# Decoder trunk on one core: the second layer's mixer norm by token on turned residual rows, top two by index instruction

## The chip, the core and the metric

The kernel runs on one NeuronCore of one Trainium2 chip. The metric is the device time of one execution in microseconds (us); lower is better. Before the change three runs gave a median of 1497.2 us (1497.12 to 1497.33).

## The reference, cut to what matters

Two layers over 288 tokens (256 of a prompt, 8 x 4 samples) of width 1024, all in float32. Layer 0 has a dense feed-forward, layer 1 routes each token to two of eight experts:

```python
h = layer_norm(ALPHA * h + mix, p['ln_mix_g'][i], p['ln_mix_b'][i])
flat = h.reshape(bsz * L, D_MODEL)
...
    f = moe_swiglu(flat, p['w_router'][j], p['w_e_gate'][j], p['w_e_up'][j], p['w_e_down'][j])
h = layer_norm(ALPHA * h + f.reshape(bsz, L, D_MODEL), p['ln_ffn_g'][i], p['ln_ffn_b'][i])
...
def moe_swiglu(h, w_router, w_gate, w_up, w_down):
    logits = (h @ w_router).astype(jnp.float32)
    top_logit, top_e = lax.top_k(logits, TOP_K)
    gates = jax.nn.softmax(top_logit, axis=-1).astype(h.dtype)
...
        return (jax.nn.silu(xb @ w_gate[e]) * (xb @ w_up[e])) @ w_down[e]
...
    return jnp.zeros((T, D), h.dtype).at[sorted_tok].add(y_assign * w_assign[:, None])
```

`layer_norm(x, g, b)` is `(x - mean) * rsqrt(var + 1e-5) * g + b` over the 1024 channels of a token.

## The kernel before

**Layout.** Activations lie channel by token: `h` and `r` are eight blocks (k) of 128 channels x 288 tokens. Every fp32 weight chunk (1 MB) comes through a ring of six buffers, loaded on SyncE's queue (SP), and is split in two fp32r halves: ScalarE (ACT) copies `w_hi`, VectorE (DVE) subtracts for `w_lo` (three slots each). TensorE (PE) multiplies hi by hi, hi by lo and lo by hi. All orders are written out by hand, engine by engine, with semaphores.

**From the second mixer to the experts** (layer 1; the place of the change). PE projects the mixer's output block by block (L691); DVE adds `ALPHA*h` to give `r` (L1393) and keeps a running sum of the blocks (L1400). Then comes a norm over channels, which lie on partitions: PE sums with a matrix of ones (L519, L523), DVE centres eight blocks (L1314), ACT squares them (L1027), PE sums the squares (L538), DVE takes the variance off the diagonal (L1377), GpSimd (POOL) takes the power of -0.5 (L2039), PE spreads the result over all partitions (L547), DVE multiplies (L1683), ACT applies the vectors g and b (L1152). PE turns the finished `h` into rows by token (L806), ACT and DVE split those into `h_tok_hi` (L1210) and `h_tok_lo` (L1749). Beside this PE computes the router's logits on the centred `r` (L793), and DVE finds the two largest with 14 small operations, each waiting for the one before (L1719 to L1740).

**Selection and gathering.** PE counts each chosen token's place in its expert (L829 to L831); DVE compares the places with a row of slot numbers (L1765), which gives `sel`, a 0/1 matrix of tokens by slots for the experts 0 and 1. PE gathers their tokens with `sel` in four pieces q of two channel blocks (L845), ACT and DVE split each piece into `x_hi` (L1218) and `x_lo` (L1884). PE starts expert 0 (item 0) when two pieces are there and its chunk 1 when all four are. `keep_warm` (L507) is a run of matmuls whose result nobody reads.

**The experts.** Each of the eight items is 42 chunks p in seven groups g. For every chunk from p = 2 ACT cuts `w_hi` (L1253), then DVE `w_lo` (L1940). The generator `extra_items` hands DVE one small piece of other work behind each cut of item 0 (`beside`): among it the sum of the two halves to plain rows `x_rows` (L1803, L1813) and the start of the result `r_tok` (L1798). POOL stores `x_rows` to DRAM (L2114), from where the later experts' tokens are fetched.

## Time and profile before

| | |
|---|---|
| median of three runs | 1497.2 us |
| the profiled execution, its own time | 1497.28 us |
| its span on the core | 1495.5 us |
| PE busy | 1481.0 us, 99% |
| DVE, ACT, POOL busy | 82%, 64%, 6% |
| granted TensorE clock, mean | 0.999 |

A span is the time from the first to the last record of the core; the execution's own time has 1.8 us more around it. An engine is busy while an instruction of it runs. A matmul's record is longer than the distance to the next one, since matmuls are pipelined, so distances between starts tell more. A wait is named by what ended it.

### The profile page before, as it was taken

What the parts mean: (1) busy time and instruction counts of PE and PEld (TensorE: products, weight loads), DVE (VectorE), ACT (ScalarE), POOL (GpSimd) and SP (SyncE); (2) the same over time, 40 slices, a digit from 0 to 9 for tenths busy, and PEclk for the clock granted to TensorE, in tenths of its full rate; (3) what the DMA queues carried; (4) which work ended last, traced back from release to release, by engine and by line L of the source; (5) the groups of instructions that cost most, each with busy time, mean ns of one, the idle gap of its engine ahead of it and who ended that gap; (6) DMA issues with size and microseconds to landing.
All of it is one profiled execution on the core that took longest, in us unless ns stands there. A gap on an engine that the chain in (4) does not pass through costs nothing.

```text
span 1495.5 us, 20554 instructions
## 1 busy us (share of the span) xinstructions
PE 1481.0 (99%) x7975; PEld 1285.3 (86%) x7975; DVE 1231.3 (82%) x1260; ACT 957.0 (64%) x891; POOL 94.8 (6%) x104
## 2 busy tenths in 40 slices
PE   9999999999999999999999999999999999999998
PEld 8989999999998788888888888888888888788887
DVE  7977655554697788899999988898889889999886
ACT  5734433344374477777777777777777777677774
POOL 3402000000021000001000000100000101100000
PEclk9999999999999999999999999999999999999999
DMA  9725544454251479999999999999999999999991
GB/s 346 160 78 190 182 158 166 169 169 169 85 130 57 169 285 399 374 390 373 421 376 369 378 390 381 392 366 375 371 366 403 375 398 380 408 371 358 379 378 69
DMA packets 68154, 439.43 MB, mean 294 GB/s; under 512 B 9504, under 2 KB 13536, under 8 KB 16608
## 3 DMA queue, kind: packets, MB, share of 16 engines
q1 hardware_dynamic: 60320, 424.68, 74.8%
q0 software_dynamic: 4816, 12.32, 2.7%
q10 hardware_dynamic: 2928, 1.18, 0.3%
q8 instruction: 63, 1.03, 0.3%
q14 instruction: 27, 0.22, 0.0%
HBM read 431.06 MB, written 7.09 MB: 293 GB/s over the span
## 4 chain that ended last, share of the span: by engine, by line
PE 94%; DVE 3%; ACT 1%; issue 1%; DMA 0%; DVEq 0%; POOL 0%; SPq 0%; ACTq 0%; POOLq 0%
PE bank L885 60%; PE bank L557 23%; PE bank L691 4%; PE bank L928 2%; PE bank L507 1%; PE bank L581 1%; DVE w_lo L1940 1%; PE bank L538 1%; DVE w_lo L1326 0%; ACT w_hi L1055 0%; PE bank L547 0%; PE bank L523 0%; PE bank L875 0%; PE bank L866 0%; DVE r L1393 0%
## 5 line engine op out<-in xcount | busy, mean ns | idle before, releaser
L1940 DVE TENSOR_TENSOR w_lo<-ring,w_hi 128x2048 fp32r<-128x2048 f32 x320 | 731.2, 2290 | 84.2 <-ACT w_hi L1253 81.7
L1253 ACT ACTIVATE w_hi<-ring 128x2048 fp32r<-128x2048 f32 x320 | 613.5, 1918 | 163.0 <-PE bank L885 163.0
L885 PE MATMUL bank<-w_hi,x_hi 128*128 128x512 f32 x896 | 354.2, 395 | 0.9 <-DVE w_lo L1940 0.8
L885 PE MATMUL bank<-w_hi,x_lo 128*128 128x512 f32 x896 | 349.6, 390 | 0.0
L885 PE MATMUL bank<-w_lo,x_hi 128*128 128x512 f32 x896 | 348.9, 389 | 0.0
L557 PE MATMUL bank<-x_hi,w_hi 128*128 128x290 f32 x664 | 199.5, 300 | 0.6 <-DVE w_lo L1326 0.5
L885 PEld LDWEIGHTS bank<-w_hi,x_lo 128*128 128x128 f32 x896 | 168.2, 188 | 35.7
L885 PEld LDWEIGHTS bank<-w_hi,x_hi 128*128 128x128 f32 x896 | 168.4, 188 | 35.3 <-issue 1.9
L557 PE MATMUL bank<-x_lo,w_hi 128*128 128x290 f32 x664 | 197.7, 298 | 0.0
L557 PE MATMUL bank<-x_hi,w_lo 128*128 128x290 f32 x664 | 197.3, 297 | 0.0
L885 PEld LDWEIGHTS bank<-w_lo,x_hi 128*128 128x128 f32 x896 | 168.5, 188 | 33.3
L1326 DVE TENSOR_TENSOR w_lo<-ring,w_hi 128x2048 fp32r<-128x2048 f32 x60 | 137.2, 2289 | 34.3 <-ACT w_hi L1055 31.3
L1055 ACT ACTIVATE w_hi<-ring 128x2048 fp32r<-128x2048 f32 x60 | 114.0, 1905 | 53.6 <-PE bank L557 44.2
L557 PEld LDWEIGHTS bank<-x_hi,w_hi 128*128 128x128 f32 x664 | 126.0, 190 | 2.0 <-DVE w_lo L1326 1.1
L557 PEld LDWEIGHTS bank<-x_lo,w_hi 128*128 128x128 f32 x664 | 126.3, 190 | 0.3
L557 PEld LDWEIGHTS bank<-x_hi,w_lo 128*128 128x128 f32 x664 | 126.0, 190 | 0.0
L885 PE MATMUL bank<-w_hi,ad_hi 128*128 128x512 f32 x256 | 100.4, 392 | 0.1
L885 PE MATMUL bank<-w_hi,ad_lo 128*128 128x512 f32 x256 | 99.8, 390 | 0.0
L885 PE MATMUL bank<-w_lo,ad_hi 128*128 128x512 f32 x256 | 99.7, 390 | 0.0
L885 PE MATMUL bank<-w_hi,odd_hi 128*128 128x512 f32 x192 | 75.6, 394 | 0.0
L885 PE MATMUL bank<-w_hi,odd_lo 128*128 128x512 f32 x192 | 74.9, 390 | 0.0
L885 PE MATMUL bank<-w_lo,odd_hi 128*128 128x512 f32 x192 | 74.8, 389 | 0.0
(300 smaller groups left out, 1759.7 us busy)
## 6 DMA issues: line engine op xcount, KB each, us to landing
ring<-in_w_e_gate SPq DMA_DIRECT2D x112, 1024.0 KB, 7.1
ring<-in_w_e_up SPq DMA_DIRECT2D x112, 1024.0 KB, 7.1
ring<-in_w_e_down SPq DMA_DIRECT2D x112, 1024.0 KB, 7.3
ring<-in_w_in SPq DMA_DIRECT2D x16, 1024.0 KB, 5.9
ring<-in_w_ff_gate SPq DMA_DIRECT2D x14, 1024.0 KB, 5.0
ring<-in_w_ff_up SPq DMA_DIRECT2D x14, 1024.0 KB, 5.0
ring<-in_w_ff_down SPq DMA_DIRECT2D x14, 1024.0 KB, 4.9
...
```

The lines of the kernel that those rows point to most:

```text
L507: mm(bank[b][:, 384:512], ones[:, :], ones[:, :], start=True, stop=True)
L538: last = mm(bank[7][:, 0:TOKENS], ones[:, :], sq[:, b, :], start=(b == 0), stop=(b == nb - 1))
L557: ins = mm(out, w, x, start=(first and n == 0), stop=(last and n == 2), skip_group_check=True)
L581: last = mm(bank[n][:, 0:TC], w_slots[w][:, at:at + P], x_parts[x][:, k, 0:TC], start=(turn == 0 and k == 0), stop=(turn == 2 and k == KB ...
L691: last = mm(bank[(6 + d) % 8][:, 0:TOKENS], ring[c % SLOTS][:, at:at + P], y[:, k, :], start=(j == 0 and kk == 0), stop=(j == KB // FPC - ...
L885: ins = mm(out, x, w[slot][:, columns], start=(first and n == 0), stop=(last and n == 2), skip_group_check=True)
L928: last = nc.tensor.transpose(bank[6][:, f * W:(f + 1) * W], gate_e[:, g % 2, f * P:(f + 1) * P], ident)
L1055: A(w_hi[n % SPLIT][:, :], ring[c % SLOTS][:, :], ACT.Copy).then_inc(hi_done, 1)
L1253: A(w_hi[(CUT0 + p) % SPLIT][:, :], ring[(START + p) % SLOTS][:, :], ACT.Copy).then_inc(hi_done, 1)
L1326: V.tensor_tensor(w_lo[n % SPLIT][:, :], ring[c % SLOTS][:, :], w_hi[n % SPLIT][:, :].bitcast(F32), ALU.subtract).then_inc(lo_done, 1)
L1940: V.tensor_tensor(w_lo[(CUT0 + p) % SPLIT][:, :], ring[(START + p) % SLOTS][:, :], w_hi[(CUT0 + p) % SPLIT][:, :].bitcast(F32), ALU.subtra ...
```

## The change

The norm of layer 1's mixer is computed by token. PE turns the plain residual `r` (neither centred nor scaled) into token rows at once (`turn_rows`), DVE takes mean and variance of each row with the batch-norm instructions (`bn_stats`, `bn_aggr`), POOL the power, and ACT writes the rows centred and scaled, without the vectors g and b (`tok_full`, into `x_rows` and, for the last 32 tokens, `gate_e`). DVE splits these SBUF rows (`tokens_high`, `tokens_low`). The router runs on plain `r`, and mean and scale enter as a bias per token and expert (`logit_bias`). The two largest logits come from the instructions `max` and `max_index`. The selection is one instruction of 768 elements. The gather order is changed: all high parts first, then the low parts. ACT applies g and b to the gathered blocks (`first_full`), and DVE splits them. For the stored rows, POOL now multiplies by g and adds b on whole 128x1024 rows (g and b are loaded for this, 1 MB), and sums the two halves of the last tile; DVE's three sums leave item 0. DVE's softmax steps move behind the first cuts of item 0.

```diff
+        tok_rows = [x_rows[:, 0, :], x_rows[:, 1, :], gate_e.rearrange("p g n -> p (g n)")]
...
-            raw_logits(0, 4)
-            next(norm)
-            raw_logits(4, KB).then_inc(logits_ready, 1)
...
+            def turn_rows(half):
+
+                pe.wait_ge(r_ready, 2 * KB + (5 if half else KB))
+                for t in range(TT):
+                    rows = TILE_ROWS[t]
+                    for j in range(4):
+                        last = nc.tensor.transpose(bank[TURN_BANKS[half][t]][0:rows, j * P:(j + 1) * P],
+                                                   r[:, 4 * half + j, t * P:t * P + rows], ident)
+                    last.then_inc(r_turned, 1)
+
+            turn_rows(1)
+            turn_rows(0)
+            for k in range(KB):
+                last = mm(bank[1][0:N_EXPERTS, 0:TOKENS], router_g[:, k, :], r[:, k, :], start=(k == 0), stop=(k == KB - 1))
+            last.then_inc(logits_ready, 1)
...
+                last = nc.tensor.transpose(bank[7][0:rows, 64 + t * 8:64 + t * 8 + 8],
+                                           logit_t[0:8, t * P:t * P + rows], ident[0:8, 0:8])
+            last.then_inc(logits_turned, 1)
+            keep_warm(1, 8)
...
+            keep_warm(1, 7)
...
+            def gather_first():
+
+                pe.wait_ge(sel_ready, 1)
+                pe.wait_ge(pad_ready, 2)
+                for blocks in (range(KB - 1), [KB - 1]):
+                    for rows, ready in ((h_tok_hi, h_tok_hi_done), (h_tok_lo, h_tok_lo_done)):
+                        for t in range(TT):
+                            pe.wait_ge(ready, 2 * t + 2)
+                            for k in blocks:
+                                last = mm(first_bank(k), rows[:, t, k * P:(k + 1) * P], sel[:, t, :],
+                                          start=(t == 0 and rows is h_tok_hi), stop=(t == TT - 1 and rows is h_tok_lo),
+                                          skip_group_check=True)
+                                if t == TT - 1 and rows is h_tok_lo and k % 2:
+                                    last.then_inc(gathered, 1)
...
-            pe.wait_ge(pad_ready, 3)
-            pe.wait_ge(h_tok_hi_done, 6)
-            pe.wait_ge(h_tok_lo_done, 2)
-            keep_warm(3, 10)
...
+            pe.wait_ge(tok_full, 6)
+            gather_first()
...
             act.wait_ge(st_v, 128)
+            act.wait_ge(mean_rstd_ready, 1)
...
-                act.wait_ge(h_turned, n + 1)
-                A(h_tok_hi[0:rows, t, half * 512:(half + 1) * 512], bank[2 + 2 * t + half][0:rows, :],
-                  ACT.Copy).then_inc(h_tok_hi_done, 1)
-
...
+                A(tok_rows[t][0:rows, half * 512:(half + 1) * 512], bank[TURN_BANKS[half][t]][0:rows, :], ACT.Identity,
+                  scale=rstd_tok[0:rows, t:t + 1],
+                  bias=less_mean_rstd[0:rows, t:t + 1]).then_inc(tok_full, 1)
...
+                for k in range(2):
+                    c = 2 * q + k
+                    last = A(gate_e[:, q % 2, k * 2 * W:(k + 1) * 2 * W],
+                             bank[min(c, 6)][:, c // 7 * 2 * W:(c // 7 + 1) * 2 * W], ACT.Identity, scale=v_at("ln_mix_g", 1, 2 * q + k),
+                             bias=v_at("ln_mix_b", 1, 2 * q + k))
+                last.then_inc(x_full, 1)
...
-            residual(2, "ffn0", D_ORDER, 2)
-            ln_centre("mix1", r)
+            residual(2, "ffn0", D_ORDER)
...
+            V.tensor_copy(router_b[:, 0:2, :], bank[7][:, 300:316].rearrange("p (a e) -> p a e", a=2)).then_inc(router_set, 1)
+            dve.wait_ge(r_turned, 1)
...
+            for half in (1, 0):
+                for t in range(TT):
+                    rows = TILE_ROWS[t]
+                    dve.wait_ge(r_turned, (0 if half else TT) + t + 1)
+                    V.bn_stats(out=row_stats[0:rows, t, 6 * half:6 * half + 6],
+                               in_=bank[TURN_BANKS[half][t]][0:rows, :]).then_inc(tok_stats, 1)
...
+                V.bn_aggr(out=row_mean_var[0:rows, t, :], in_=row_stats[0:rows, t, :]).then_inc(tok_stats, 1)
+            dve.wait_ge(tok_stats, 2 + 3 * TT)
+            V.tensor_scalar(var_tok[:, :], row_mean_var[:, :, 1], LN_EPS, None, ALU.add).then_inc(mix_var, 1)
...
+                    V.tensor_copy(h_tok_hi[at], full).then_inc(h_tok_hi_done, 1)
...
+                    V.tensor_tensor(h_tok_lo[at], full, h_tok_hi[at].bitcast(F32), ALU.subtract).then_inc(h_tok_lo_done, 1)
...
+            V.scalar_tensor_tensor(out=less_mean_rstd[:, :], in0=row_mean_var[:, :, 0], scalar=-1.0, in1=rstd_tok[:, :],
...
+                last = V.scalar_tensor_tensor(out=logit_bias[:, t, :], in0=router_b[:, 1, :], scalar=less_mean_rstd[:, t:t + 1],
+                                              in1=router_b[:, 0, :], op0=ALU.mult, op1=ALU.add)
+            step(last)
             dve.wait_ge(logits_ready, 1)
-            V.tensor_copy(logit_t[0:N_EXPERTS, :], bank[0][0:N_EXPERTS, 0:TOKENS]).then_inc(logits_out, 1)
-            ln_scale_mix1(4, 7)
+            V.tensor_copy(logit_t[0:N_EXPERTS, :], bank[1][0:N_EXPERTS, 0:TOKENS]).then_inc(logits_out, 1)
+            tokens_high(0)
...
-                V.tensor_reduce(best, values, AX_X, ALU.max).then_inc(chosen_top, 1)
...
-                    lambda: V.tensor_reduce(col[:, 7, :], key[:, :, :], AX_X, ALU.max),
-                    lambda: V.tensor_tensor(hot, key[:, :, :], over_experts(col[:, 7, :]), ALU.is_equal),
...
-            step(V.scalar_tensor_tensor(out=logit[:, :, :], in0=hot1[:, :, :], scalar=-3.0e38, in1=logit[:, :, :],
-                                        op0=ALU.mult, op1=ALU.add))
-            top(logit[:, :, :], hot2[:, :, :], col[:, 1, :])
...
+            for t in range(TT):
+                last = V.max(out=top_value[:, t, :], in_=logit[:, t, :])
+            step(last)
+            for t in range(TT):
+                last = V.max_index(out=top_index[:, t, :], in_max=top_value[:, t, :], in_values=logit[:, t, :])
+            step(last)
+            step(V.tensor_copy(top_no[:, :, :], top_index[:, :, 0:2]))
+            step(V.tensor_tensor(hot[:, :, :, :],
...
+            V.tensor_tensor(chosen[:, :, :], hot1, hot2, ALU.add).then_inc(chosen_ready, 1)
+            V.tensor_tensor(col[:, 2, :], top_value[:, :, 1], top_value[:, :, 0], ALU.subtract).then_inc(top_diff, 1)
+            tokens_high(1, 2)
...
-            select(slice(0, 1), slice(1, 2))
-            tokens_low(1, 4, 3, 5)
...
+            V.tensor_tensor(sel[:, :, :].rearrange("p t (e n) -> p t e n", e=2),
+                            const("slot").unsqueeze(1).unsqueeze(1).broadcast_to([P, TT, 2, W]),
+                            item_pos[:, :, 0:2].unsqueeze(3).broadcast_to([P, TT, 2, W]), ALU.is_equal).then_inc(sel_ready, 1)
+            tokens_high(3, 4, 5)
+            tokens_low(*range(6))
             item_g = item_gate[:, :, 0:N_EXPERTS]
-            step(V.tensor_tensor(item_g, hot1[:, :, :], over_experts(col[:, 4, :]), ALU.mult))
-            step(V.tensor_tensor(hot2[:, :, :], hot2[:, :, :], over_experts(col[:, 5, :]), ALU.mult))
...
+                dve.wait_ge(x_full, q + 1)
+                full = gate_e[:, q % 2, :].rearrange("p (k e n) -> p e k n", k=2, e=2)
+                V.tensor_copy(xs_hi[:, :, 2 * q:2 * q + 2, :], full).then_inc(x_hi_done, 1)
+                dve.wait_ge(x_hi_done, q + 1)
+                V.tensor_tensor(xs_lo[:, :, 2 * q:2 * q + 2, :], full, xs_hi[:, :, 2 * q:2 * q + 2, :].bitcast(F32),
+                                ALU.subtract).then_inc(x_lo_done, 1)
...
-                    pool.wait_ge(st_v, 64 * DEPTH)
-                    pool.wait_ge(ln_xn, OUT_AT["mix1"] + KB)
-                    for v in (h_tok_hi, h_tok_lo, sel):
+                    for s in (st_a, st_c, st_d, st_v):
+                        pool.wait_ge(s, 64 * DEPTH)
+                    for n in range(2):
+                        G.dma_start(y_rows[n][:, :], t_in["mix_gb"][n]).then_inc(gb_in, 16)
+                    pool.wait_ge(r_turned, 1)
+                    for v in (h_tok_hi, h_tok_lo):
                         G.memset(v[:, 2, :].bitcast(F32), 0.0).then_inc(pad_ready, 1)
-                    pool.sem_inc(y_rows_free, 2)
+                    pool.wait_ge(mix_var, 1)
+                    G.tensor_tensor(rstd_tok[:, :], var_tok[:, :], minus_half[:, :], ALU.pow).then_inc(mix_rstd, 1)
+                    pool.wait_ge(pad_ready, 2)
+                    pool.wait_ge(gb_in, 32)
                     for t in range(TT):
+                        pool.wait_ge(h_tok_lo_done, 2 * t + 2)
+                        if t == 2:
+                            pool.wait_ge(r_start, 1)
+                            pool.wait_ge(rows_out, 32)
+                            G.tensor_tensor(x_rows[:, 0, :], h_tok_hi[:, 2, :].bitcast(F32), h_tok_lo[:, 2, :].bitcast(F32),
+                                            ALU.add).then_inc(rows_part, 1)
+                            pool.wait_ge(rows_part, 3)
+                        to = x_rows[:, t % 2, :]
+                        G.tensor_tensor(to, to, y_rows[0][:, :], ALU.mult).then_inc(rows_part, 1)
+                        pool.wait_ge(rows_part, t + 1 + t // 2)
+                        rows = TILE_ROWS[t]
+                        G.tensor_tensor(x_rows[0:rows, t % 2, :], x_rows[0:rows, t % 2, :], y_rows[1][0:rows, :],
+                                        ALU.add).then_inc(rows_staged, 1)
                         pool.wait_ge(rows_staged, t + 1)
                         G.dma_start(token_rows[t * P:(t + 1) * P, :], x_rows[:, t % 2, :]).then_inc(rows_out, 16)
+                    pool.sem_inc(y_rows_free, 2)
```

The order of the instructions at the two places of which the prediction speaks. First DVE from the copy of the router's sums to the first of the logits. In these names `ybuf` holds all the small router tiles, `bs` the router's vectors, `bank` is PSUM. Before:

```order
L1678 COPY bs<-bank 128x8
L1377 ISA ybuf,var_tok<-bank,cst 128x128
L1377 ISA var_tok 128x1
L1377 ISA ybuf,var_tok<-bank,cst 128x128
L1377 ISA var_tok 128x1
L1377 ISA ybuf,var_tok<-bank,cst 32x32
L1377 ISA var_tok 32x1
L1683 TENSOR_TENSOR h<-r,bank 128x288 x4
L1700 MEMSET ybuf 128x24
L1702 COPY ybuf<-bank 8x288
L1683 TENSOR_TENSOR h<-r,bank 128x288 x3
L1709 SCALAR_TENSOR_TENSOR ybuf<-bank,rstd_tok,bs 128x8 x2
```

The same engine and place now:

```order
L1700 BN_STATS ybuf<-bank 128x6 x2
L1700 BN_STATS ybuf<-bank 32x6
L1700 BN_STATS ybuf<-bank 128x6 x2
L1700 BN_STATS ybuf<-bank 32x6
L1705 BN_AGGR ybuf<-ybuf 128x2 x2
L1705 BN_AGGR ybuf<-ybuf 32x2
L1707 TENSOR_SCALAR var_tok<-ybuf 128x3
L1739 SCALAR_TENSOR_TENSOR ybuf<-ybuf,rstd_tok 128x3
L1744 SCALAR_TENSOR_TENSOR ybuf<-bs,ybuf 128x8 x3
L1748 COPY ybuf<-bank 8x288
L1730 CAST h_tok_hi<-x_rows 128x512
L1753 SCALAR_TENSOR_TENSOR ybuf<-bank,rstd_tok,ybuf 128x8 x2
```

The diagonal reads and the eight products of 288 columns are gone; six statistics of 512 columns stand there.

Second, POOL from the clearing of the padding to the first store of the rows' last tile. Before:

```order
L2110 MEMSET h_tok_hi 128x1024
L2110 MEMSET h_tok_lo 128x1024
L2110 MEMSET sel 128x256
L2114 DMA token_rows<-x_rows 128x1024 x3
L2130 DMA token_rows<-y_rows_61 128x1024
```

Now (`y_rows_61` and `y_rows_62` hold g and b at this time):

```order
L2139 TENSOR_TENSOR rstd_tok<-var_tok,minus_half 128x3
L2151 TENSOR_TENSOR x_rows<-x_rows,y_rows_61 128x1024
L2154 TENSOR_TENSOR x_rows<-x_rows,y_rows_62 128x1024
L2157 DMA token_rows<-x_rows 128x1024
L2151 TENSOR_TENSOR x_rows<-x_rows,y_rows_61 128x1024
L2154 TENSOR_TENSOR x_rows<-x_rows,y_rows_62 128x1024
L2157 DMA token_rows<-x_rows 128x1024
L2147 TENSOR_TENSOR x_rows<-h_tok_hi,h_tok_lo 128x1024
L2151 TENSOR_TENSOR x_rows<-x_rows,y_rows_61 128x1024
L2154 TENSOR_TENSOR x_rows<-x_rows,y_rows_62 32x1024
L2157 DMA token_rows<-x_rows 128x1024
```

POOL has seven operations on rows of 1024 that it did not have.

## Rows read from the trace of the kernel before

**Rows 1.** Page part 4, chain by engine; part 5: line, busy us, mean ns, idle us.
```profile
PE 94%; DVE 3%; ACT 1%; issue 1%; DMA 0%; DVEq 0%; POOL 0%; SPq 0%; ACTq 0%; POOLq 0%
...
L1940 DVE TENSOR_TENSOR w_lo<-ring,w_hi 128x2048 fp32r<-128x2048 f32 x320 | 731.2, 2290 | 84.2 <-ACT w_hi L1253 81.7
```

**Rows 2.** Busy us (instructions) by stretch, then PEclk, DMA share, GB/s.
```profile
460.00:480.00 20.00, 20.00 (x106) 16.66 (x105) 15.23 (x41) 4.00 (x4) 0.38 (x1) 1.00 0.01 1
...
541.80:559.11 17.31, 17.21 (x77) 13.76 (x76) 17.31 (x12) 12.41 (x8) 1.15 (x2) 1.00 0.97 371
559.11:575.90 16.79, 16.79 (x78) 13.91 (x77) 15.59 (x10) 12.40 (x8) 0.00 (x0) 1.00 1.01 416
```

**Rows 3.** Timeline of PE around layer 1's second norm: start us, us, operation.
```profile
482.50 13.85 PE L691 MATMUL bank<-ybuf,ring 128*128 128x288 f32 x56
...
498.68 4.15 PE L538 MATMUL bank<-ybuf,ones 128*128 128x288 f32 x16 [0.90 <-ACT ybuf L1027]
502.76 2.11 PE L793 MATMUL bank<-r,bs 128*8 128x288 f32 x8
...
512.55 2.84 PE L507 MATMUL bank<-ones 128*128 128x128 f32 x24
515.23 0.30 PE L829 MATMUL bank<-ybuf,cst 128*128 128x24 f32 x2
```

**Rows 4.** Timeline of DVE, same stretch.
```profile
496.39 0.46 DVE L1393 SCALAR_TENSOR_TENSOR r<-h,bank 128x288 f32<-128x288 f32 x1
...
509.86 0.48 DVE L1709 SCALAR_TENSOR_TENSOR ybuf<-bank,rstd_tok,bs 128x8 f32<-128x8 f32 x3 [0.34 <-PE bank L815]
...
510.62 0.16 DVE L1719 TENSOR_REDUCE ybuf<-ybuf 128x3 f32<-128x24 f32 x1
...
513.19 0.18 DVE L1740 TENSOR_TENSOR ybuf<-ybuf,cst 128x24 f32<-128x24 f32 x1
...
516.00 0.18 DVE L1756 SCALAR_TENSOR_TENSOR ybuf<-bank,ybuf 128x24 f32<-128x24 f32 x1 [1.23 <-PE bank L831]
...
517.62 2.46 DVE L1749 TENSOR_TENSOR h_tok_lo<-bank,h_tok_hi 128x512 fp32r<-128x512 f32 x4
...
524.57 0.69 DVE L1884 TENSOR_TENSOR x_lo<-bank,x_hi 128x512 fp32r<-128x512 f32 x1 [1.38 <-ACT x_hi L1218]
```

**Rows 5.** Timeline of PE: the first matmul of the experts.
```profile
525.18 0.39 PE L885 MATMUL bank<-w_hi,x_hi 128*128 128x512 f32 x1
```

**Rows 6.** Groups by line and form, DVE: busy us, mean ns, idle.
```profile
L1798 DVE TENSOR_SCALAR r_tok<-x_rows 128x1024 f32<-128x1024 f32 x3 | 2.1, 687 | 0.0
L1803 DVE TENSOR_TENSOR x_rows<-h_tok_hi,h_tok_lo 128x1024 f32<-128x1024 f32 x2 | 2.4, 1219 | 0.0
```

**Rows 7.** The same, ACT.
```profile
L1300 ACT ACTIVATE h<-bank,vec 128x288 f32<-128x288 f32 x4 | 2.0, 589 | 3.7 <-PE bank L1010 3.7
```

**Rows 8.** Groups by form, POOL: busy us, mean ns, idle.
```profile
L2110 POOL MEMSET h_tok_hi<- 128x1024 f32 x1 | 1.0, 951 | 6.4 <-DVE h L1683 6.4
L2041 POOL MEMSET w_pool<- 128x512 f32 x1 | 0.5, 524 | 0.3 <-POOLq L2216 0.3
```

**Rows 9.** Timelines of POOL and DVE where both work at once, and where not.
```profile
47.99 0.81 POOL L2065 TENSOR_SCALAR_AFFINE_SELECT ws_t<-ws_t 128x512 f32<-128x512 f32 x1
...
48.22 0.85 DVE L1533 SCALAR_TENSOR_TENSOR work<-ext_a,vec,work 128x256 f32<-128x256 f32 x1
...
49.44 1.18 POOL L2073 TENSOR_SCALAR_AFFINE_SELECT ws_s<-ws_s 32x256 f32<-32x256 f32 x1
...
49.75 0.98 DVE L1533 SCALAR_TENSOR_TENSOR work<-ext_a,vec,work 128x256 f32<-128x256 f32 x1
...
52.77 2.27 DVE L1326 TENSOR_TENSOR w_lo<-ring,w_hi 128x2048 fp32r<-128x2048 f32 x1
...
53.29 2.52 POOL L2039 TENSOR_TENSOR rstd_tok<-var_tok,minus_half 128x3 f32<-128x3 f32 x1
...
503.56 0.85 POOL L2039 TENSOR_TENSOR rstd_tok<-var_tok,minus_half 128x3 f32<-128x3 f32 x1 [22.18 <-DVE var_tok L1377]
```

275 lines of the change are left out of this document (123 added, 152 removed).

## The prediction

> **What bounds the kernel now.** I read the chain of waits first: PE holds 94% of it, and the costliest neighbours of PE's matmuls are DVE's cuts of the weights, 2.29 us each [rows 1]. So the experts run at PE's pace, and time is to be had only where PE waits or does work that feeds nobody. Next the table by stretches: within the experts a group, a seventh of an item, takes 16.79 us, DVE is busy for 15.59 of it; in the second group of item 0 it takes 17.31 us and DVE is busy for all 17.31 [rows 2]. DVE has 1.2 us to spare in a group, and none where it has extra work. The timelines give the place of the change. PE's last projection ends at 482.50 + 13.85 = 496.35, DVE's last piece of `r` at 496.39 + 0.46 = 496.85 [rows 3, 4], the experts' first matmul starts at 525.18 [rows 5]. Between them lie 28.3 us of norm, router, selection and gather. Everything behind moves with that start, if DVE keeps up.
>
> **Part one, the path from `r` to the first expert matmul, as if POOL disturbed nobody.**
> DVE's running sums vanish; they stood beside PE's projections, which end at 496.35 whatever DVE does, so this is worth nothing. PE turns `r` at once: 24 transposes of 128 columns, priced as the keep-warm passes (24 in 2.84 us, 0.12 each [rows 3]), 496.4 to 499.3. The six statistics read 512 columns of PSUM. No row shows this instruction; the nearest is the subtraction that reads the same bank, four in 2.46, 0.615 each [rows 4], and with it DVE goes from 497.1 to 500.9. If the instruction takes no more than a 288-column one (0.46 [rows 4]) it is 1 us less, if it passes twice over its data 3.7 us more. Four small ones at 0.2 follow: variance at 501.7. POOL's power takes 0.85 [rows 9], with the hand-over: 502.6, and the small product 502.8. Meanwhile PE does the logits on plain `r`, two rows like the one of 2.11 us [rows 3], 499.3 to 503.5. So PE's logits and DVE's statistics end together, each covers the other, and a slower statistic costs only what it exceeds 0.7 us by. Copy 0.45, transposes 0.5, three products 0.48: logits at 505.0. Before, they were there at 509.86 + 0.48 = 510.34 [rows 4]: 5.3 us sooner.
>
> The top two took from 510.62 to 513.19 + 0.18 = 513.37, 2.75 us for 13 operations, 0.21 each [rows 4]. Now there are nine, 1.9 us: chosen at 506.9. `max` and `max_index` are in no row; at 0.1 or at 0.4 each the six move this by -0.6 or +1.2 us. I take 0.21, as all DVE's small operations have. Next the counts. Before, 24 keep-warm passes ran to 512.55 + 2.84 = 515.4 and the counting matmul started only at 515.23 [rows 3], 1.9 us after the choice was made at 513.37; DVE idled 1.23 us for it and started at 516.00 [rows 4]. Now 16 passes end at 506.4, before the choice. From the counting matmul to DVE it took 516.00 - 515.23 = 0.77: 507.7, two small steps 508.3. The selection is one instruction of 768 elements: 1.219 for 1024 with two SBUF inputs [rows 6] less 0.27 for a quarter is 0.95, 509.2. It was finished at 517.62 [rows 4]: 8.4 us sooner.
>
> What stood behind the selection gets longer. Before, the high parts were done by then, and four low parts ran beside PE's gathering. Now DVE copies three high parts after it. A one-input operation on 1024 takes 0.687 [rows 6], half of that length 0.42, with 0.36 from start to start: 510.3. Six low parts at 0.61: 514.0. PE follows with the high parts under this cover; the first piece is gathered at 514.4. ACT now needs two operations per piece with both vectors (0.589 for 288 columns [rows 7]; 0.5 from start to start, 1.05 a piece), and DVE two, 0.42 and 0.69 (the latter in [rows 4]). Piece 0 is split at 516.7, piece 1 at 517.8, and there the experts start: 7.3 us sooner than 525.18 [rows 5]. Pieces 2 and 3 come at 520.1, before chunk 1 wants them a chunk later (16.79 / 6 = 2.8 us with its turn). Further on, DVE's two sums of 1.22 [rows 6] leave the saturated second group, and 7 small steps of 0.2 enter, most of them earlier. I count 0.5 us, the whole excess of 17.31 over 16.79 [rows 2]. Sum of part one: -7.8 us. The load of g and b, 1 MB, is issued near 481, where the DMA engines rest (share 0.01 [rows 2]); I cost it at nothing.
>
> **Part two, what POOL takes back.** POOL now does seven operations on rows of 1024: multiply and add for tile 0 and tile 1, behind the second and fourth low part, then sum, multiply, add for tile 2 in item 0. Does this disturb DVE? In two places of this trace both work on SBUF at once. At 48.22 DVE needs 0.85 us for 256 columns, at 49.75 0.98, each beside a select of POOL; by the slope between 1219 for 1024 [rows 6] and 2290 for 2048 [rows 1] such an operation takes 0.44. So DVE stood still for 0.4 and 0.5 us, until 0.2 us before the select's end. And POOL's power, 0.85 when DVE rests, takes 2.52 beside a cut that runs 52.77 to 55.04: it waited for the cut's end [rows 9]. One at a time, then, at least when DVE has two inputs in SBUF, as the low parts, the splits (now from SBUF, formerly from PSUM) and all cuts have.
> This is what the Trainium skill states (SBUF — State Buffer, Who interferes with whom): a DVE instruction with two SBUF inputs and a GpSimd one that reads SBUF exclude each other for the whole instruction, and so do one-input copies in a two-port mode. The trace agrees, by the 0.85 and 0.98 us. Without the rule the sum would be -7.8 us, with it about 0.
>
> How long is one? The clearing of 1024 takes 0.951, of 512 0.524 [rows 8]: 0.43 more for 512. A select of 512, one input, takes 0.81 [rows 9], so 1024 with one input 1.24. If the second input is read after the first, 0.85 more: 2.1. Ends 1.24 and 2.1. I take 2.1, since both inputs must be read and the select, the nearest row, already pays one. It stands in DVE's way for 1.9.
> The Trainium skill (GPSIMD Engine Reference, Elementwise — side-by-side cycle accounting) gives 4497 ns for an fp32 add of 2048, and calls it a floor for two inputs; half is 2.25, an estimate, by which the sum below would be 1 us higher. No row here shows it.
>
> The first four: from 511.6, when the second low part is done, to the start of the experts DVE's work is on the path except the 1.5 us in which it waits for the first piece (514.0 to 515.5) and gaps of 0.8 us together. 4 x 1.9 = 7.6, less 2.3: +5.3 us. The first expert matmul starts at about 523.2, and the gathering and the first pieces are late, not the router. The last three start when DVE has begun `r_tok`, chunk 8 of item 0, about 546, where DVE has no reserve. 3 x 1.9 = 5.7; in those 14 us DVE can spare 1.0, does 1.2 us of products and splits with a PSUM input beside POOL, and is 0.7 us ahead of PE: +2.8 us of PE waiting for `w_lo`. Sum: -7.8 + 5.3 + 2.8 = +0.3 us. The profiled execution took 1497.28 (span 1495.5 and 1.8 around it), 0.1 over the median; so 1497.5 for the median.
>
> **Rivals.**
> (a) POOL costs nothing: it fits in DVE's gaps or reads in short bursts. For it: DVE waits 1.38 us for ACT within the splits as before [rows 4]; against it the two stretched operations of [rows 9]. It gives -7.8: 1489.4.
> (b) POOL's operations are short, 1.24 us, 1.0 in DVE's way: 4.0 less 2.3 is 1.7, and in item 0 3.0 less 2.9: nothing. -7.8 + 1.8 = -6; with some of the gaps missed, -4: 1491 to 1493.
> (c) Slower: DVE starves the experts. The mechanism is (b)'s reverse: a POOL operation of more than 2.4 us. Each 0.1 us adds 0.7 over seven of them, since all cover is used up. At 2.5: +0.3 + 2.8 = +3.1, 1500.3. For it: POOL's power of three columns already takes 0.85 [rows 9]. PE standing idle for some microseconds between gather and experts would add to it if the clock fell; the granted clock reads 1.00 in all stretches shown [rows 2], and no row has such an idle time.
> (d) The router path is longer than I make it (statistics passing twice, dear index instructions): up to +3 us on part one, the same on the sum. I count it half within my forecast, half with (c).
> (e) The change doesn't shorten the path, because PE's passes and not DVE's choice set the counting: excluded, since the passes now end before the choice even by 0.4 us.
>
> **How the numbers follow.** Forecast 0.44 (1494.5 to 1500.1 its own range), (a) 0.17, (b) 0.18, (c) with (d) 0.21. What a measurement can tell from no change is 0.2%, 3 us. Faster by that holds (a) and (b): 0.35. Same 0.44. Slower 0.21. The range leaves out the far end of (a) and of (c): 1489.6 to 1501.0.
>
> **What would show it.** Right: DVE's variance near 501.7, choice near 507, selection near 509 in the new timeline; low parts or splits of DVE recorded with 2 us and more instead of 0.69, beside POOL's multiply and add of about 2.1; the first expert matmul near 523; the second and third groups of item 0 longer than 16.79. Wrong: POOL records under 1.5 us, DVE splits at 0.7, first expert matmul at 518; or the choice later than 509. If POOL's and DVE's operations overlap at their full speed, my second part falls as a whole.

## The result, and the profile after

The changed kernel takes 1501.58 us (median of six runs, 1501.19 to 1504.24) against 1497.28 for the kernel before (1497.12 to 1497.39): ratio 1.0032, 95% interval 1.0020 to 1.0044. It is slower by 4.3 us, 0.6 us beyond the far end of the range. The six executions lie further apart than those before, and the longest (1504.24) has the lowest mean granted clock, 0.994 against 0.996 and 0.997, so what is said below of the clock holds for the profiled executions alone. The profiled execution has a span of 1499.9 us, 4.4 more than 1495.5.

The page of the changed kernel answers to [rows 1]: the chain by engine, and DVE's cuts (busy us, mean ns, idle us). DVE has gone from 3% to 5% of the chain, a cut from 2290 to 2308 ns in the mean, and the cuts as a whole from 731.2 to 737.2 us.

```profile
PE 92%; DVE 5%; issue 1%; ACT 1%; DMA 0%; DVEq 0%; POOL 0%; SPq 0%; ACTq 0%; POOLq 0%
...
L1963 DVE TENSOR_TENSOR w_lo<-ring,w_hi 128x2048 fp32r<-128x2048 f32 x320 | 737.2, 2308 | 85.2 <-ACT w_hi L1267 82.4
```

Timeline of DVE from `r` to the splits, as [rows 4] (start us, us, operation). Down to the selection (L1797, ended 508.5) all of it is sooner than before. Then three low parts (L1736) last 2.84, 2.84 and 3.40 instead of 0.67.

```profile
498.17 2.46 DVE L1700 BATCH_NORM_STATS2 ybuf<-bank 32x6 f32<-32x512 f32 x4
...
500.92 0.17 DVE L1707 TENSOR_SCALAR var_tok<-ybuf 128x3 f32<-128x3 f32 x1
...
504.71 0.30 DVE L1758 MAX8 ybuf<-ybuf 128x8 f32<-128x8 f32 x3
...
505.40 0.16 DVE L1761 FIND_INDEX8 ybuf<-ybuf 128x8 uint32<-128x8 f32 x1
...
506.03 0.18 DVE L1768 TENSOR_TENSOR ybuf<-ybuf 128x24 f32<-128x24 f32 x1
...
507.57 0.96 DVE L1797 TENSOR_TENSOR sel<-cst,ybuf 128x768 fp32r<-128x768 f32 x1
...
510.06 0.67 DVE L1736 TENSOR_TENSOR h_tok_lo<-x_rows,h_tok_hi 128x512 fp32r<-128x512 f32 x1
...
511.26 2.84 DVE L1736 TENSOR_TENSOR h_tok_lo<-x_rows,h_tok_hi 128x512 fp32r<-128x512 f32 x1
...
514.03 2.84 DVE L1736 TENSOR_TENSOR h_tok_lo<-work,h_tok_hi 32x512 fp32r<-32x512 f32 x1
...
516.79 3.40 DVE L1736 TENSOR_TENSOR h_tok_lo<-work,h_tok_hi 32x512 fp32r<-32x512 f32 x1
522.14 0.57 DVE L1915 CAST x_hi<-work 128x512 fp32r<-128x512 f32 x1 [1.94 <-ACT work L1223]
```

POOL in the same stretch and in item 0. Each of the three long low parts ends 0.55 us after one of POOL's first three operations (513.55, 516.32 and 519.64), about the time that a low part takes by itself (0.67, 0.60 from start to start). The fourth runs almost wholly while DVE waits 1.94 us for ACT anyway. With 2.35 us the third shows what one takes when it has no wait of its own in it.

```profile
510.90 2.65 POOL L2151 TENSOR_TENSOR x_rows<-x_rows,y_rows 128x1024 f32<-128x1024 f32 x1 [8.85 <-DVE h_tok_lo L1736]
513.63 2.69 POOL L2154 TENSOR_TENSOR x_rows<-x_rows,y_rows 128x1024 f32<-128x1024 f32 x1
...
517.29 2.35 POOL L2151 TENSOR_TENSOR x_rows<-x_rows,y_rows 128x1024 f32<-128x1024 f32 x1
519.72 2.71 POOL L2154 TENSOR_TENSOR x_rows<-x_rows,y_rows 128x1024 f32<-128x1024 f32 x1
...
548.08 4.33 POOL L2147 TENSOR_TENSOR x_rows<-h_tok_hi,h_tok_lo 128x1024 f32<-128x1024 f32 x1 [24.75 <-DVE r_tok L1808]
552.49 4.32 POOL L2151 TENSOR_TENSOR x_rows<-x_rows,y_rows 128x1024 f32<-128x1024 f32 x1
556.89 4.32 POOL L2154 TENSOR_TENSOR x_rows<-x_rows,y_rows 32x1024 f32<-32x1024 f32 x1
```

The third low part is a case by itself: it stands still from its start at 516.79, half a microsecond before the third operation begins, 3.40 - 0.67 = 2.73 us in all against 2.84 - 0.67 = 2.17 for the other two. POOL issues its first store there (516.62 to 517.26). No run here shows why; in experiment 1 a low part keeps its pace beside such an issue.

PE waits for the low parts, 1.93 and 4.24 us, and starts the experts at 525.04, 0.14 us sooner than [rows 5]. In item 0 it waits three times for a cut.

```profile
514.15 1.86 PE L855 MATMUL bank<-sel,h_tok_lo 128*128 128x256 f32 x7 [1.93 <-DVE h_tok_lo L1736]
520.25 1.86 PE L855 MATMUL bank<-sel,h_tok_lo 128*128 128x256 f32 x7 [4.24 <-DVE h_tok_lo L1736]
...
525.04 0.48 PE L896 MATMUL bank<-w_hi,x_hi 128*128 128x512 f32 x1
...
554.70 0.47 PE L896 MATMUL bank<-w_hi,x_hi 128*128 128x512 f32 x1 [1.39 <-DVE w_lo L1963]
...
559.01 0.50 PE L896 MATMUL bank<-w_hi,x_hi 128*128 128x512 f32 x1 [1.34 <-DVE w_lo L1963]
...
563.42 0.50 PE L896 MATMUL bank<-w_hi,x_hi 128*128 128x512 f32 x1 [0.91 <-DVE w_lo L1963]
```

DVE in item 0. The two engines take turns: POOL's sum at 548.08 waits until the cut of 547.85 is over, the cut of 550.85 until the sum is over, and so on, 4.3 to 4.5 us for what takes 2.3. The multiplication at 550.24, which has one input in PSUM, runs in its usual 0.69 in the middle of POOL's sum.

```profile
547.85 2.29 DVE L1963 TENSOR_TENSOR w_lo<-ring,w_hi 128x2048 fp32r<-128x2048 f32 x1
...
550.24 0.69 DVE L1945 TENSOR_TENSOR work<-work,bank 128x512 f32<-128x512 f32 x1
550.85 3.71 DVE L1963 TENSOR_TENSOR w_lo<-ring,w_hi 128x2048 fp32r<-128x2048 f32 x1
...
554.48 4.48 DVE L1963 TENSOR_TENSOR w_lo<-ring,w_hi 128x2048 fp32r<-128x2048 f32 x1
```

By stretches (columns as in [rows 2]): the granted clock is 0.52 and 0.56 around PE's idle time, so mostly at its lower level of 1.2 GHz, and the second and third groups of item 0 take 20.12 and 18.21 us instead of 17.31 and 16.79. The fourth is back at 16.78. From there on the whole program is 4.2 to 4.4 us late.

```profile
514.00:520.00 6.00, 1.86 (x7) 1.57 (x7) 6.00 (x3) 0.00 (x0) 5.60 (x4) 0.52 0.22 87
520.00:525.00 5.00, 4.75 (x25) 4.75 (x25) 2.91 (x6) 3.35 (x7) 3.03 (x2) 0.56 0.22 89
...
541.79:561.91 20.12, 17.39 (x77) 13.72 (x76) 20.02 (x13) 12.39 (x8) 13.38 (x4) 1.00 0.85 314
561.91:580.12 18.21, 17.30 (x78) 13.86 (x77) 17.16 (x11) 12.49 (x8) 0.19 (x1) 1.00 0.96 351
```

So the two traces say: nothing won at the start of the experts, and 4.2 us lost in item 0. What they can't say is how much the router path had won before POOL took it back, and whether the loss ahead of the experts is POOL's alone or in part that of the half clock (the 0.52 and 0.56 above).

### The profile page after: what moved, and what is told of

The parts are those of the page before. It is cut to its first block, busy times and chain, and to the rows that moved or that the text cites. A ratio compares the mean times of both kernels' runs of the same rounds, so it can differ in the third digit from the quotient of the medians.

```text
span 1499.9 us, 20479 instructions
## 1 busy us (share of the span) xinstructions
PE 1478.1 (99%) x7945; PEld 1283.1 (86%) x7945; DVE 1238.3 (83%) x1249; ACT 952.4 (63%) x879; POOL 120.4 (8%) x112
## 4 chain that ended last, share of the span: by engine, by line
PE 92%; DVE 5%; issue 1%; ACT 1%; DMA 0%; DVEq 0%; POOL 0%; SPq 0%; ACTq 0%; POOLq 0%
PE bank L896 58%; PE bank L570 23%; PE bank L704 4%; DVE w_lo L1963 2%; PE bank L937 2%; PE bank L520 1%; PE bank L594 1%; DVE h_tok_lo L1736 1%; PE bank L551 0%; DVE w_lo L1340 0%; ACT w_hi L1064 0%; ACT w_hi L1267 0%; PE bank L886 0%; PE bank L877 0%; DMA h<-in_x_t 0%
## 5 line engine op out<-in xcount | busy, mean ns | idle before, releaser
L1963 DVE TENSOR_TENSOR w_lo<-ring,w_hi 128x2048 fp32r<-128x2048 f32 x320 | 737.2, 2308 | 85.2 <-ACT w_hi L1267 82.4
```

Source lines behind the costliest of these rows:

```text
L1963: V.tensor_tensor(w_lo[(CUT0 + p) % SPLIT][:, :], ring[(START + p) % SLOTS][:, :], w_hi[(CUT0 + p) % SPLIT][:, :].bitcast(F32), ALU.subtra ...
```

## Experiments

Line numbers are those of each kernel. The times of the kernel before were 1497.3 us beside all of them.

**1. Without the six operations on g and b.**

```diff
-                        G.tensor_tensor(to, to, y_rows[0][:, :], ALU.mult).then_inc(rows_part, 1)
+                        pool.sem_inc(rows_part, 1)
...
-                        G.tensor_tensor(x_rows[0:rows, t % 2, :], x_rows[0:rows, t % 2, :], y_rows[1][0:rows, :],
-                                        ALU.add).then_inc(rows_staged, 1)
+                        pool.sem_inc(rows_staged, 1)
```

> Edit: POOL's six multiplications and additions of g and b on the stored rows are left out (so the experts' later inputs and the residual rows lack g and b); the sum of tile 2 in item 0, the stores and all waits on them stay. In the changed kernel these six are recorded with 2.65, 2.69, 2.35, 2.71, 4.32 and 4.32 us, and DVE's low parts beside them with 2.84, 2.84 and 3.40 instead of 0.67. Theory L (one of DVE and POOL works on SBUF at a time): the first expert matmul comes at 517.8, as part one of the prediction has it, 7.2 us sooner than the 525.04 of the changed kernel; of the 4.3 us that item 0 loses, the sum keeps about 1. Time 1501.6 - 7.2 - 3.3 = 1491. Rival C (half of the loss ahead of the experts is PE's: it idles 4.24 us and then gathers at a granted clock of 0.50 to 0.56): the same here, since PE does not idle either. Rival R (the path of router, selection and splits is longer than part one has it, and the lock hides it): first expert matmul at 520 or later, time 1493 or more.

1490.95 us, ratio to before 0.9958 (0.9944 to 0.9972). DVE's last low part ends at 512.71 + 0.67 = 513.38 and not at 520.19, the experts start at 517.31. Timelines of DVE and PE:

```profile
512.71 0.67 DVE L1736 TENSOR_TENSOR h_tok_lo<-work,h_tok_hi 32x512 fp32r<-32x512 f32 x1
```

```profile
517.31 0.51 PE L896 MATMUL bank<-w_hi,x_hi 128*128 128x512 f32 x1 [0.81 <-DVE x_lo L1917]
```

Theory L, and rival R is out: the new path is 7.87 us shorter than the old one (525.18 - 517.31) when nobody disturbs it. Item 0's two groups take 35.20 us together with only the sum in them, against 38.33.

**2. Without tile 2's three operations in item 0.**

```diff
-                            G.tensor_tensor(x_rows[:, 0, :], h_tok_hi[:, 2, :].bitcast(F32), h_tok_lo[:, 2, :].bitcast(F32),
-                                            ALU.add).then_inc(rows_part, 1)
+                            pool.sem_inc(rows_part, 1)
...
+                        if t == 2:
+                            pool.sem_inc(rows_part, 1)
+                        else:
+                            G.tensor_tensor(to, to, y_rows[0][:, :], ALU.mult).then_inc(rows_part, 1)
```

> Edit: only the last three of POOL's seven operations go, sum, multiplication and addition for tile 2 in item 0 (its 32 stored rows are then wrong); waits and stores stay. Theory L: ahead of the experts nothing changes, first expert matmul at 525.0 +- 0.2. Item 0's second and third group go back from 20.12 and 18.21 us to 16.8 each (17.31 and 16.79 before the change), all its cuts of DVE to 2.29. Time 1501.6 - 4.5 = 1497.1. Rival R2 (item 0 is late for another reason, such as ACT's splits or the 4 KB reads and writes of rows by DMA): the second group stays above 18 us and the time above 1499.

1497.26 us (1496.99 to 1499.91), ratio 1.0006 (0.9997 to 1.0015): the median is what was expected, to 0.2 us. The experts start at 524.92, and the stretches of the second and third group are

```profile
541.71:558.75 17.04, 17.04 (x77) 13.81 (x76) 16.25 (x14) 12.42 (x8) 0.53 (x1) 1.00 1.00 391
558.75:575.54 16.79, 16.79 (x77) 13.90 (x76) 15.47 (x10) 12.41 (x8) 0.00 (x0) 1.00 1.00 393
```

The whole loss of item 0 is POOL's three operations, 38.33 - 33.83 = 4.5 us; rival R2 is out.

**3. The first four later.**

```diff
                         pool.wait_ge(h_tok_lo_done, 2 * t + 2)
+                        if t == 0:
+                            pool.wait_ge(x_lo_done, 4)
```

> Edit: one more wait on POOL ahead of its first multiplication, until DVE has split the first pair of inputs (fourth low part); nothing is left out. The four operations then stand beside item 0's first cuts. Theory L: first expert matmul at 517.8. Four operations of 2.35 us now hold DVE in item 0's first group, where it waits for 0.58 + 0.32 + 0.34 + 1.35 = 2.6 us in all: 9.4 - 2.6 = 6.8 us of PE waiting for w_lo there. Time 1501.6 - 7.2 + 6.8 = 1501.2, so the same as the changed kernel. Rival C (a good part of the loss ahead of the experts is the half clock after PE's idle time): PE does not idle ahead of the experts now, so this part is won: 1499 or less.

1500.59 us, ratio 1.0022 (1.0013 to 1.0031). The experts start at 517.13, 7.9 us sooner, and the first group then takes 540.65 - 517.13 = 23.5 us where 16.75 is usual: 6.8 us of waiting, as worked out. Theory L; the cost moves along with POOL's operations. Of the changed kernel's 1501.58 only 1 us is saved, where rival C had at least 2.6. In DVE's timeline even an operation of 128x3 with a single input takes 2.35 us, so it stands for the whole of POOL's addition (it ends at 526.38, POOL's at 526.36). In the changed kernel, where POOL rests at that place, the same operation takes 0.16. First this kernel's DVE, then its POOL, then DVE of the changed kernel:

```profile
520.03 4.08 DVE L1963 TENSOR_TENSOR w_lo<-ring,w_hi 128x2048 fp32r<-128x2048 f32 x1 [0.58 <-ACT w_hi L1267]
524.03 2.35 DVE L1811 TENSOR_SCALAR ybuf<-ybuf 128x3 f32<-128x3 f32 x1
```

```profile
522.04 4.32 POOL L2156 TENSOR_TENSOR x_rows<-x_rows,y_rows 128x1024 f32<-128x1024 f32 x1
```

```profile
529.67 0.16 DVE L1811 TENSOR_SCALAR ybuf<-ybuf 128x3 f32<-128x3 f32 x1
```

**4 and 5. PE kept busy in its waits.** First with 14 and 28 calls of `keep_warm`, then with 7 and 20. The edit of the second:

```diff
+                            if len(blocks) > 1 and rows is h_tok_lo and t:
+                                keep_warm(7, (0, 7, 20)[t])
                             pe.wait_ge(ready, 2 * t + 2)
```

> Edit: PE does 14 dummy passes of 128 columns ahead of its wait for the low part of tile 1 and 28 ahead of that of tile 2, so it does not rest in the 1.93 and 4.24 us; nothing is left out. Theory L: the low part of tile 2 still ends at 520.2 with POOL in its way. The granted clock stays 1.00 instead of 0.50 to 0.56 between 514 and 524; the gathering behind it takes half as long, ACT starts 0.3 to 0.5 us sooner, and the first expert matmul waits for DVE's second split: 524.3. Time 1500.8. Rival C (the clock bears the 2 us by which my first term fell short): first expert matmul at 523.0, time 1499.5.

1502.94 us, ratio 1.0038 (1.0024 to 1.0052): a miss by my own fault. A call is two passes, so the 56 passes ran to 522.66, and the gathering started 2.2 us late. The clock stayed at 1.00 throughout, and the start was at 526.26.

> Edit: the changed kernel with PE kept busy in its two waits by 7 and 20 dummy calls (14 and 40 passes of 0.117 us: 1.65 and 4.7 us), so that they end before the low parts do; the last attempt's 56 passes took 6.41 us and held the gathering back until 522.42. Nothing is left out. Theory L: DVE's low part of tile 2 ends at 520.2, the gathering behind it runs at full clock, ACT starts at 520.8 instead of 521.09, DVE's second split ends at 523.9 instead of 524.4; the first expert matmul follows 0.3 to 0.8 us sooner than 525.04; time 1500.8 to 1501.3. Rival C (the half clock behind PE's idle time bears 2 us of the loss): first expert matmul at 523.0, time 1499.5.

1503.01 us, ratio 1.0039 (1.0025 to 1.0052): slower, not faster. The start did come 0.37 us sooner. But now the clock fell after it, in the experts' first matmuls, the first group took 18.42 us instead of 16.75, and the first turn of item 0 was at 543.09 instead of 541.79. Timelines of PE and DVE and the stretches of this kernel:

```profile
524.67 0.50 PE L898 MATMUL bank<-w_hi,x_hi 128*128 128x512 f32 x1 [1.29 <-DVE x_lo L1919]
```

```profile
521.93 0.89 DVE L1917 CAST x_hi<-work 128x512 fp32r<-128x512 f32 x1 [1.65 <-ACT work L1225]
```

```profile
514.00:520.00 6.00, 5.56 (x47) 5.37 (x47) 6.00 (x3) 0.00 (x0) 5.60 (x4) 1.00 0.23 90
524.67:530.00 5.33, 5.33 (x16) 4.25 (x17) 4.59 (x7) 3.45 (x4) 0.00 (x0) 0.68 0.11 45
```

Rival C is out: with PE at full clock from 509 to 524 the start is at 524.67, not at 523.0. From the end of the last low part to the start the changed kernel takes 525.04 - 520.19 = 4.85 us, experiment 1 takes 517.31 - 513.38 = 3.93. Of these 0.92 us the run at full clock keeps 0.46, and they are those by which its first cast is longer beside POOL's fourth operation (0.89 us; 0.57 in the changed kernel, 0.43 in the run without the six). So the half clock costs the changed kernel 0.5 us ahead of the experts; as it delays the cast, most of the fourth operation is over by then, and the two losses hide each other in part. Why the clock falls behind some waits and not behind others (none in the run without the six, which idles 0.81 us) these runs don't settle.

**6. One input instead of two.**

```diff
-                        G.tensor_tensor(to, to, y_rows[0][:, :], ALU.mult).then_inc(rows_part, 1)
+                        G.tensor_scalar(to, to, 1.0, None, ALU.mult).then_inc(rows_part, 1)
```

(and `+ 0.0` for the addition)

> Edit: each of POOL's six multiplications and additions is an operation with one input, rows times 1 or plus 0, of the same 1024 columns (g and b are left out of the stored rows); the sum for tile 2 keeps its two inputs. Theory L with the price by inputs: POOL's operation takes 1.24 us, as my second bound had it (a select of 512 columns took 0.81, the clearing shows 0.43 for 512 more), and DVE stands still for each. Without the six the first expert matmul came at 517.31, with two-input ones of 2.35 at 525.04: 7.7 lost of 9.4, so 1.7 covered. With 1.24: 5.0 - 1.7 = 3.3, first expert matmul at 520.6; in item 0 two of 1.24 and the sum: 1 + 1.5 us. Time about 1491 + 3.3 + 1.5 = 1495.8. Rival N: POOL's size on 1024 is not set by the number of inputs (arithmetic costs as much as two reads): 2.3 us again, and the time is that of the changed kernel, 1501.

1493.99 us, ratio 0.9978 (0.9969 to 0.9987): neither. The operation is not shorter but longer, 2.83 us; yet it holds DVE for a part of that only. Timelines of POOL and DVE:

```profile
511.20 3.05 POOL L2151 TENSOR_SCALAR x_rows<-x_rows 128x1024 f32<-128x1024 f32 x1 [8.89 <-DVE h_tok_lo L1736]
...
518.19 2.82 POOL L2151 TENSOR_SCALAR x_rows<-x_rows 128x1024 f32<-128x1024 f32 x1
```

```profile
511.54 1.51 DVE L1736 TENSOR_TENSOR h_tok_lo<-x_rows,h_tok_hi 128x512 fp32r<-128x512 f32 x1
512.98 0.67 DVE L1736 TENSOR_TENSOR h_tok_lo<-work,h_tok_hi 32x512 fp32r<-32x512 f32 x1
...
518.21 1.35 DVE L1915 CAST x_hi<-work 128x512 fp32r<-128x512 f32 x1
519.59 0.69 DVE L1917 TENSOR_TENSOR x_lo<-work,x_hi 128x512 fp32r<-128x512 f32 x1
520.20 1.09 DVE L1915 CAST x_hi<-work 128x512 fp32r<-128x512 f32 x1
521.33 1.40 DVE L1917 TENSOR_TENSOR x_lo<-work,x_hi 128x512 fp32r<-128x512 f32 x1
```

At the beginning of a POOL operation the low part stretches by 0.84, a cast by 0.92 and the split at 521.33 by 0.71 (POOL's next operation starts at 521.09). The two-input ones behind them, at 512.98 and 519.59, run free although POOL is busy to 514.25 and 521.01; only a cast near the end, at 520.20, is stretched again, by 0.66. So both of my models of a POOL operation, its length by inputs and a hold for all of its length, fail for this kind.

**7. Writing only.**

```diff
-                        G.tensor_tensor(to, to, y_rows[0][:, :], ALU.mult).then_inc(rows_part, 1)
+                        G.memset(to, 0.25).then_inc(rows_part, 1)
```

> Edit: each of the six is a memset of the same 1024 columns (so the stored rows are constants); the sum for tile 2 stays. Theory L as the two stretched operations of rows 9 have it (POOL's selects both read and write): whether a POOL operation that reads nothing holds DVE is open. If it does (L1): 0.95 us each (rows 8), low parts stretched by that, first expert matmul at 517.3 + 3.8 - 1.7 = 519.4, time 1493 to 1494. If it does not (L2): the low parts stay at 0.67, first expert matmul at 517.3, time 1491.0 as without the six operations.

1491.71 us, ratio 0.9966 (0.9954 to 0.9978), 0.8 us more than without the six: L2 for the low parts, all six of which keep their pace (four in 2.48 us) with two memsets beside them (511.15 to 513.11); the third falls into DVE's wait for ACT. The 0.8 us are one cast, SBUF to SBUF with one input, that starts with POOL's fourth memset and takes 1.21 instead of 0.43. DVE's timeline, then POOL's:

```profile
509.73 2.48 DVE L1736 TENSOR_TENSOR h_tok_lo<-x_rows,h_tok_hi 128x512 fp32r<-128x512 f32 x4
...
515.06 1.21 DVE L1915 CAST x_hi<-work 128x512 fp32r<-128x512 f32 x1 [1.65 <-ACT work L1223]
```

```profile
515.04 0.95 POOL L2154 MEMSET x_rows<- 128x1024 f32 x1
```

The Trainium skill (SBUF — State Buffer, Who interferes with whom) has it so: DVE with two SBUF inputs collides with a GpSimd instruction that reads SBUF, not with one that only writes; a cast in a two-port mode collides with either; with one SBUF input and outside those modes there is no collision. The traces agree: here 0.67 beside memsets and 1.21 for the cast, in the changed kernel 0.69 for L1945 beside the sum. The section of the Trainium skill also has it that the shared ports are locked for the whole instruction. For POOL's operations with two inputs the traces agree (2.17 of 2.35 us), for those of experiment 6 they don't.

**8. Half the width.** The six work on columns 0 to 511.

```diff
-                        G.tensor_tensor(to, to, y_rows[0][:, :], ALU.mult).then_inc(rows_part, 1)
+                        G.tensor_tensor(to[:, 0:512], to[:, 0:512], y_rows[0][:, 0:512], ALU.mult).then_inc(rows_part, 1)
```

> Edit: POOL's six multiplications and additions work on the first 512 of the 1024 columns (the second half of the stored rows goes without g and b); the sum keeps its width. Theory L: size and hold go with the width, 1.2 us instead of 2.35 each, and DVE stands still for that. Ahead of the experts four of them cost 4.8 less 1.7 of cover, first expert matmul at 517.3 + 3.1 = 520.4. In item 0 the two wide ones cost 38.33 us for two groups against 35.20 without them, 3.1 us; narrow ones about 1.2. Time 1491.0 + 3.1 + 1.2 = 1495.3; by the slope of the prediction's third rival (0.1 us in an operation is 0.7 us in the time, 0.6 for six) 1501.6 - 6.9 = 1494.7. Rival F (an operation has a high fixed cost, or holds DVE for a fixed time as the one-input operation did, 0.8 us each of its 2.83): the time does not follow the width; with a fixed hold of 2.35 1500 or more, with 0.8 1493 to 1494.

1496.17 us (1495.85 to 1498.90), ratio 0.9997 (0.9988 to 1.0006): 0.9 us above the estimate, rival F out. Timelines of POOL and DVE:

```profile
515.30 1.27 POOL L2151 TENSOR_TENSOR x_rows<-x_rows,y_rows 128x512 f32<-128x512 f32 x1
```

```profile
514.81 2.32 DVE L1736 TENSOR_TENSOR h_tok_lo<-work,h_tok_hi 32x512 fp32r<-32x512 f32 x1
```

The start is at 521.63, and item 0's two groups take 574.47 - 538.39 = 36.08 us. Over six operations the time moved by 1501.58 - 1496.17 = 5.4 us for 6 x 1.08 us of length: 0.83 us per us, where rival (c) had reckoned with 1. This third low part again stands still 0.56 us longer than the two before it (2.32 - 0.67 = 1.65 us against 1.76 - 0.67 = 1.09), so that part of the hold does not follow the width.

**9. DVE does the rows itself.** The edit that the others point to: DVE's 1.22 us for 1024 columns instead of a hold of 2.35, in pieces where it has time. Three things change at once: DVE does POOL's seven operations, ACT takes over the start of `r_tok`, and six small steps of DVE move ahead of the experts.

```diff
+        START_AT = [(0, 16), (0, 28), (1, 6)]
...
+                            A(r_tok[:, t, :], x_rows[:, t % 2, :], ACT.Copy, scale=ALPHA).then_inc(r_start, 1)
...
+                        for half in range(2):
+                            c = slice(512 * half, 512 * half + 512)
...
+                                V.tensor_tensor(x_rows[:, t % 2, c], x_rows[:, t % 2, c], y_rows[0][:, c],
+                                                ALU.mult).then_inc(rows_part, 1)
...
+                                V.tensor_tensor(x_rows[0:rows, t % 2, c], x_rows[0:rows, t % 2, c], y_rows[1][0:rows, c],
+                                                ALU.add).then_inc(rows_staged, 1)
...
-                        G.tensor_tensor(to, to, y_rows[0][:, :], ALU.mult).then_inc(rows_part, 1)
```

> Edit: nothing of the computation is left out. DVE does the sum, the multiplications and the additions of g and b on the stored rows, in 14 halves of 512 columns, one at every second or third chunk of item 0; POOL only issues the stores; ACT starts the three rows of r_tok (DVE 0.69 us each before); DVE's six small gate steps move from item 0 into its wait for the first gathered piece (1.65 us in the run without the six operations). Theory L: the loss is POOL's 2.35 us a piece in which DVE stands still; DVE does the same work in 1.22 us for 1024 columns with two SBUF inputs (rows 6), so 0.65 a half. First expert matmul at 517.3 as in the run without the six. In item 0 DVE gets 14 x 0.65 = 9.1 us, less 2.1 for r_tok and 1.2 for the small steps that it gives away: 5.8 net, against 1.2 us to spare in each of seven groups. Nothing or little is lost there: 1501.6 - 7.7 - 4.3 = 1489.6, up to 1491. Rival Q: DVE falls behind all the same, since what is spare in a group can't be saved for another (it is only three cuts ahead of PE): PE waits for w_lo in several groups, 1493 or more.

1489.96 us, ratio 0.9951 (0.9937 to 0.9964): faster than both kernels, 7.35 us below the one before and 11.6 below the changed one. The experts start at 517.29, and item 0 runs at PE's pace although DVE is busy for 16.50 of 16.79 us:

```profile
534.00:550.79 16.79, 16.79 (x77) 13.87 (x76) 16.50 (x13) 12.41 (x8) 0.60 (x1) 1.00 1.00 382
```

What each of the three changes is worth by itself no run shows.

**10. The old choice of the top two, in that version.**

```diff
-            for t in range(TT):
-                last = V.max(out=top_value[:, t, :], in_=logit[:, t, :])
...
+            top(logit[:, :, :], hot1, col[:, 0, :])
+            step(V.scalar_tensor_tensor(out=logit[:, :, :], in0=hot1, scalar=-3.0e38, in1=logit[:, :, :],
+                                        op0=ALU.mult, op1=ALU.add))
+            top(logit[:, :, :], hot2, col[:, 1, :])
```

> Edit: in the version in which DVE applies g and b and POOL only stores (1489.96 us), the choice of the top two is made in the old way again, 13 operations of DVE in a chain instead of max, max_index, a cast, a comparison and an addition. Nothing is left out. The chain takes 2.75 us by the rows of before (0.21 each), the new way took 1.50 (504.71 to 506.21). Theory P (this version's start of the experts hangs on the choice, as part one of the prediction has it): selection, low parts and first expert matmul 1.25 us later, 518.5 instead of 517.3, time 1491.2. Rival S: the start hangs on DVE's and ACT's splits or on PE's passes, and the later choice is absorbed: 1490.0, and in the changed kernel the index instructions were worth nothing.

1492.16 us (1490.97 to 1492.67), ratio 0.9965 (0.9951 to 0.9978). The start moves from 517.29 to 518.61, 1.32 us, as theory P has it. The time is 1 us above its 1491.2: another 0.9 us arises in item 0, where PE now waits 0.57 us for a cut (51.23 us from the first to the fourth turn against 50.36). That DVE is so full there that small shifts count is my reading; no run tests it.

## Why the prediction was wrong

The mechanism was the forecast one, POOL and DVE excluding each other. What failed is what part two of the prediction paid for it: the length of a POOL operation, which was taken too short and counts seven times, and the cover that was to hide it, which was taken too large. The first is 2 us of the 4 us by which the sum fell short. Step by step:

- **Path from `r` to the choice.** Right. Variance forecast for 501.7, recorded at 501.09; choice 506.9, recorded 506.21; selection 509.2, recorded 508.53. The statistics take 0.67 each, 0.60 from start to start (0.615 assumed). `max` and `max_index` are the part that no row showed: 0.10 and 0.17 each, 0.85 for the six (504.71 to 505.56) where 1.26 was assumed and the lower bound was 0.66.
- **-7.3 us for the start if POOL disturbed nobody.** Right: -7.87 in experiment 1, sooner by the 0.7 us of the choice. The choice's own share is confirmed by experiment 10. Of the 0.5 us more for the second group 0.27 is there when POOL rests (17.04 in experiment 2).
- **"If the second input is read after the first, 0.85 more: 2.1."** This is the step that failed. One operation takes 2.35 us, and where the prediction has it 1.9 us in DVE's way, a low part is held for 2.17 and a cut for 2.19. Seven times 0.28 is 2.0 us. The bound below was built from a select and a clearing, and the value from them as well, though neither has two inputs; experiment 6 shows that such parts don't add up. The estimate from the Trainium skill (GPSIMD Engine Reference, Elementwise — side-by-side cycle accounting), 2.25, was the nearer one; the measured 2.35 agrees with it to 0.1 us.
- **+5.3 us ahead of the experts.** 7.73 measured (525.04 - 517.31), 2.4 more. The holds are 2.17 + 2.17 + 2.73 = 7.07 us; the low parts began 0.25 sooner than in experiment 1 (509.45 against 509.70), and 0.92 arise behind them, of which 0.46 vanish at full clock (experiment 5). The 2.4 are made up of the length (4 x 0.27 = 1.1), the longer hold of the third low part (0.56), which no row of before showed and no run explains, the clock (0.5), which the forecast had only in a rival, and the cover: DVE's wait for the first piece hid 2.17 - 0.46 = 1.7 us of the fourth operation, and nothing hid the other three, where the forecast had 2.3 (0.6 more). The 0.25 of the sooner start go off. The forecast's 0.8 us of gaps was not there for POOL: from 509.45 to 520.19 DVE goes from one low part to the next.
- **+2.8 us in item 0.** 4.5 measured (experiment 2), 4.2 against [rows 2]. The three cuts are held for 1.42 + 2.19 + 2.19 = 5.80 us, and PE lost 4.5 of them. I had 5.7 less 1.2 of products with a PSUM input, so 4.5 held, and 1.7 of it spared. Of the 1.7 us between 2.8 and 4.5 the length is 3 x 0.29 = 0.9; the rest is that only one such product ran beside POOL (0.7 us) and that DVE's reserve was 1.3 us.
- **The sum.** -7.9 + 7.7 + 4.2 = +4.0 us, and 0.3 that accrue in the first group and the next items, against -7.8 + 5.3 + 2.8 = +0.3. It came nearest to rival (c), a longer POOL operation with a clock that falls in PE's idle time. But (c) began at 2.4 us, and 2.35 by its slope of 0.7 us per 0.1 gives 0.3 + 1.75 = 2.1 us, 1499.3, still inside the range. So the length alone explains half of the miss; the rest is the third low part, the clock and the cover, for which the range left no room.

Rivals (a) and (b) are refuted by the trace itself. Of the list of what would show it, variance, choice and selection came within 0.7 us; the low parts of over 2 us and the longer groups in item 0 came too. POOL's operations took 2.35 us instead of about 2.1, and the start came at 525.04 instead of near 523.
